# Sums of squares of keys and queries as two-part products with ones, with keys loaded in front of decays and a new engine order, in a delta-rule and stick-breaking trunk

## What is computed

```python
def l2_normalize(x):
    return x * lax.rsqrt(jnp.sum(x * x, axis=-1, keepdims=True) + EPS)
...
q = l2_normalize(heads(qkv[..., :GDN_WIDTH]))
k = l2_normalize(heads(qkv[..., GDN_WIDTH:2 * GDN_WIDTH]))
...
o = gated_delta_chunked(q, k, v, g, beta)
```

## Time and profile before

| what | value |
|---|---|
| median of 3 runs | 3022.31 us (3021.44 to 3025.32) |
| the profiled execution's own time | 3021.47 us |
| its span in the trace | 3019.8 us |
| PE busy | 2962.4 us, 98% |
| PEld busy | 2680.4 us, 89% |
| DVE, ACT, POOL busy | 1499.2, 851.0, 446.1 us |
| chunk loop in the trace | from 405 us to about 757 us |
| one iteration of it | 33.4 us |

### The profile page before, as it was taken

The page is one execution under the profiler, slowest core; times in us unless marked ns, Lnnn a source line. Parts: engine busy times, 40 slices in busy tenths (PEclk is TensorE's granted clock), DMA queues, the critical chain, the costliest instruction groups (busy, mean ns, idle before and its releaser), DMA issues.

```text
span 3019.8 us, 47053 instructions
## 1 busy us (share of the span) xinstructions
PE 2962.4 (98%) x19124; PEld 2680.4 (89%) x19124; DVE 1499.2 (50%) x2161; ACT 851.0 (28%) x1521; POOL 446.1 (15%) x505
## 2 busy tenths in 40 slices
PE   8999989999999999999999999999999999999998
PEld 7999978888999999999999997788888888888887
DVE  5777437666434444434346443666643433333434
ACT  4211235555221111111113102566612111111112
POOL 2000145664210000000000001000021000000000
PEclk9999989999999999999999999999999999999999
DMA  3333321121121111111111425555111111111111
GB/s 122 92 92 94 112 72 59 58 65 57 41 63 42 49 42 42 45 52 49 42 49 57 141 85 168 136 116 116 38 49 56 50 47 49 49 49 44 46 42 70
DMA packets 201815, 207.31 MB, mean 69 GB/s; under 512 B 8363, under 2 KB 172348, under 8 KB 201676
## 3 DMA queue, kind: packets, MB, share of 16 engines
q1 hardware_dynamic: 191098, 167.05, 19.1%
q0 software_dynamic: 10368, 38.21, 3.7%
q10 hardware_dynamic: 210, 0.07, 0.0%
HBM read 162.87 MB, written 42.44 MB: 68 GB/s over the span
## 4 chain that ended last, share of the span: by engine, by line
PE 95%; ACT 2%; issue 1%; DVE 1%; POOL 0%; DMA 0%; ACTq 0%; SPq 0%; DVEq 0%; POOLq 0%
PE PS L1833 20%; PE PS L1835 20%; PE PS L1834 20%; PE PS L2264 5%; PE PS L2263 5%; PE PS L2262 5%; PE PS L2385 2%; PE PS L2369 2%; PE PS L2047 1%; PE PS L2027 1%; PE PS L2336 1%; PE PS L2335 1%; PE PS L1974 1%; PE PS L2084 1%; PE PS L2074 1%
## 5 line engine op out<-in xcount | busy, mean ns | idle before, releaser
L1833 PE MATMUL PS<-YH,WL 128*128 128x348 f32 (+1 forms) x3040 | 1039.9, 342 | 4.4 <-DVE WL L1264 3.0
L1834 PE MATMUL PS<-YL,WH 128*128 128x348 f32 (+1 forms) x3040 | 1038.8, 342 | 0.0
L1835 PE MATMUL PS<-YH,WH 128*128 128x348 f32 (+1 forms) x3040 | 1038.3, 342 | 0.0
L1833 PEld LDWEIGHTS PS<-YH,WL 128*128 128x128 f32 x3040 | 572.0, 188 | 45.3 <-DVE WL L1264 3.3
L1834 PEld LDWEIGHTS PS<-YL,WH 128*128 128x128 f32 x3040 | 571.8, 188 | 37.9 <-issue 0.8
L1835 PEld LDWEIGHTS PS<-YH,WH 128*128 128x128 f32 x3040 | 572.8, 188 | 35.7
L1658 DVE TENSOR_TENSOR hT<-PS,hT 128x346 f32<-128x346 f32 (+2 forms) x440 | 251.4, 585 | 178.7 <-PE PS L2264 178.6
L803 POOL TENSOR_TENSOR gact<-gact,rs 128x346 f32<-128x346 f32 (+2 forms) x110 | 118.7, 1079 | 1307.1 <-ACT gact L1106 1307.1
L2262 PE MATMUL PS<-AH,WL 128*128 128x346 f32 (+2 forms) x880 | 308.6, 351 | 1.1 <-DVE AL L1648 1.1
L2264 PE MATMUL PS<-AH,WH 128*128 128x346 f32 (+2 forms) x880 | 308.8, 351 | 0.0
L2263 PE MATMUL PS<-AL,WH 128*128 128x346 f32 (+2 forms) x880 | 308.8, 351 | 0.0
(11 more groups left out here) (283 smaller groups left out, 3702.0 us busy)
## 6 DMA issues: line engine op xcount, KB each, us to landing
raw<-in_ffn_w_gate_up SPq DMA_DIRECT2D x88, 512.0 KB, 3.7
raw<-in_ffn_w_down SPq DMA_DIRECT2D x44, 512.0 KB, 3.6
s_in<-obuf POOLq DMA_DIRECT2D x32, 520.0 KB, 4.4
raw<-in_gdn_w_in SPq DMA_DIRECT2D x32, 512.0 KB, 4.2
Xqk<-s_in SPq DMA_DIRECT2D x10, 832.0 KB, 5.9
raw<-in_w_kv SPq DMA_DIRECT2D x16, 512.0 KB, 3.9
Xv<-s_in SPq DMA_DIRECT2D x10, 416.0 KB, 3.3
gBc<-s_g SPq DMA_DIRECT2D x10, 416.0 KB, 4.3
```

The costliest lines, as they stand in the source:

```text
L1833: pe.matmul(PS[:, bank, 0:n], wl, xh, start=(k == 0), stop=False)
L1834: pe.matmul(PS[:, bank, 0:n], wh, xl, start=False, stop=False)
L1835: m = pe.matmul(PS[:, bank, 0:n], wh, xh, start=False, stop=(k == KT - 1))
```

## The change

Sums of squares. For chunks h = 1 to 9 the two float32 products are replaced by four fp32r products. ACT writes sqh, the high part of the squares (an fp32r tile), straight from Xqk; POOL squares as before and then subtracts sqh, which leaves the low part sql; PE multiplies both parts by onesr, an fp32r tile of ones, and adds them up in PSUM. Chunk 0, whose sums are made beside the input projections, keeps the old products. Through the nested `ExitStack` sql[0] and sql[1] lie on the bytes of sq[0] and sq[1], and sqh lies on the bytes of rr. So `squares_high` waits for the `unit` that reads rr last.

Loads. SP issues Xqk of a chunk in front of gBc.

Order. The lists of POOL, ACT, DVE and PE are written anew. No other operation is added or removed.

```diff
@@ tiles
+            with ExitStack() as b:
+                sql = [b.enter_context(nc.sbuf_tensor(f"sql{g}", [128, 2, GW], F32R)) for g in range(2)]
+                sqh = b.enter_context(nc.sbuf_tensor("sqh", [128, 2, GW], F32R))
             sq = [head_only(f"sq{g}", [128, 2, GW]) for g in range(2)]
             rr = head_only("rr", [128, 2, GW])
...
+            onesr = gdn_const("onesr", [128, 128], F32R)
@@ SP
             for c in range(1, NC):
                 for g in range(2):
+                    sp.wait_ge(cs["kn"][g], c)
+                    sp.wait_ge(cs["sq"][g], c)
+                    if c > 1:
+                        sp.wait_ge(cs["shi"][g], c - 1)
+                sp.dma_start(Xqk[:, :, :], s_in[c, :, 0:16 * C].rearrange("p (t j) -> p t j", j=C)).then_inc(c_load, 16)
+                for g in range(2):
                     sp.wait_ge(cs["eg"][g], c)
                     sp.wait_ge(cs["dm"][g], c)
                 sp.dma_start(gBc[:, :, :], s_g[c:c + 1].broadcast_to([128, 8, C])).then_inc(c_gb, 16)
-                for g in range(2):
-                    sp.wait_ge(cs["kn"][g], c)
-                    sp.wait_ge(cs["sq"][g], c)
-                sp.dma_start(Xqk[:, :, :], s_in[c, :, 0:16 * C].rearrange("p (t j) -> p t j", j=C)).then_inc(c_load, 16)
@@ POOL
+            def squares_low(h, g):
+
+                pool.wait_ge(cs["sq"][g], h + 1)
+                pool.wait_ge(cs["shi"][g], h)
+                pool.tensor_tensor(sql[g][:, :, :], sq[g][:, :, :], sqh[:, :, :].bitcast(F32), ALU.subtract).then_inc(cs["slo"][g], 1)
@@ ACT
+            def squares_high(h, g):
+
+                act.wait_ge(c_load, 16 * (h + 1))
+                if g:
+                    act.wait_ge(cs["kn"][0], h + 1)
+                else:
+                    act.wait_ge(cs["kn"][1], h)
+                src = Xqk[:, :, :].rearrange("p (w h) j -> p w h j", w=2)[:, :, HG * g:HG * g + HG, :]
+                act.activation(sqh[:, :, :].rearrange("p w (h j) -> p w h j", h=HG), src, ACT.Square).then_inc(cs["shi"][g], 1)
...
+            act.activation(onesr[:, :], ones[:, :], ACT.Copy)
+
             for c in range(-1, NC + 1):
@@ PE, key_sums
-                pe.matmul(PS[:, b0, 0:GW], ones[:, :], sq[g][:, 0, :], start=True, stop=True)
-                pe.matmul(PS[:, b0 + 1, 0:GW], ones[:, :], sq[g][:, 1, :], start=True, stop=True).then_inc(cs["ss"][g], 1)
+                if h == 0:
+                    pe.matmul(PS[:, b0, 0:GW], ones[:, :], sq[g][:, 0, :], start=True, stop=True)
+                    pe.matmul(PS[:, b0 + 1, 0:GW], ones[:, :], sq[g][:, 1, :], start=True, stop=True).then_inc(cs["ss"][g], 1)
+                    return
+                pe.wait_ge(cs["slo"][g], h)
+                for w in range(2):
+                    pe.matmul(PS[:, b0 + w, 0:GW], onesr[:, :], sqh[:, w, :], start=True, stop=False)
+                    m = pe.matmul(PS[:, b0 + w, 0:GW], onesr[:, :], sql[g][:, w, :], start=False, stop=True)
+                m.then_inc(cs["ss"][g], 1)
```

More of the change, by code:

```diff
@@ L753, in _ @@
                     mask(c, 2, 1)
+                if head and h:
+                    squares_low(h, 0)
+                if levels:
+                    decayed(c, 1, 0)
+                    decayed(c, 0, 1)
+                    decayed(c, 1, 1)
+                    mask(c, 3, 0)
                     mask(c, 3, 1)
-                    decayed(c, 1, 1)
-                    mask(c, 5, 0)
+                if head and h:
+                    squares(h, 1)
+                    squares_low(h, 1)
                 if tail and t < NC - 1:
@@ L762, in _ @@
                     fade(t, 1)
[L763 to L766, removed]
                 if levels:
                     mask(c, 5, 1)
+                    mask(c, 5, 0)
+                    mask(c, 6, 1)
                     mask(c, 6, 0)
@@ L1546, in _ @@
                 if levels:
-                    add_u(c, 3, 1)
-                if head and h:
-                    unit(h, 1)
-                if head:
-                    scores(h, 0)
+                    add_u(c, 2, 1)
+                if tail and t < NC - 1:
+                    state(t, 0)
+                    state(t, 1)
                 if levels:
@@ L1555, in _ @@
                     lo(0, P_GO.job0 + 1)
+                if head and h:
+                    unit(h, 1)
+                if levels:
+                    add_u(c, 3, 1)
                 if head:
-                    scores(h, 1)
+                    scores(h, 0)
+                if tail:
+                    gated(t, 1)
                 if levels:
-                    add_u(c, 4, 1)
                     add_u(c, 4, 0)
@@ L2145, in _ @@
                     go_chunk(*GO_ORDER[2])
-                if levels:
-                    level_u(c, 0, 0)
-                    level_x(c, 1, 1)
                 if head and h:
@@ L2151, in _ @@
                 if levels:
-                    level_u(c, 1, 1)
+                    level_x(c, 1, 0)
+                    level_x(c, 1, 1)
                 if tail:
                     outputs(t, 0)
+                if tail and t < NC - 1:
+                    to_state(t, 0)
                 if levels:
-                    level_x(c, 2, 1)
-                    level_x(c, 1, 0)
+                    level_u(c, 1, 1)
+                    level_u(c, 1, 0)
                 if tail:
@@ L2173, in _ @@
                 if levels:
-                    level_u(c, 3, 1)
-                    level_u(c, 2, 0)
-                if head:
-                    key_products(h, 0)
+                    level_u(c, 2, 1)
+                    level_x(c, 3, 0)
+                    level_x(c, 3, 1)
                 if c == NC:
@@ L2182, in _ @@
                 if levels:
-                    level_x(c, 3, 0)
+                    level_u(c, 3, 0)
                 if tail:
@@ L2188, in _ @@
                 if levels:
+                    level_u(c, 3, 1)
+                if head:
+                    key_products(h, 0)
+                if levels:
                     level_x(c, 4, 1)
-                    level_u(c, 3, 0)
+                    level_x(c, 4, 0)
                 if head:
@@ L2193, in _ @@
                 if levels:
-                    level_x(c, 4, 0)
+                    level_u(c, 4, 0)
                     level_u(c, 4, 1)
```

118 lines of the change are left out of this document (54 added, 64 removed).

## The result

The changed kernel takes 3040.14 us (median of 16 runs, 3028.27 to 3052.6), the kernel before 3022.89 beside it (16 runs, 3016.15 to 3025.32): ratio 1.0062, 95% interval 1.0051 to 1.0073. It is slower by 17 us; forecast were 3011 and a range of 3003 to 3018.

The account below looks back on a forecast made before the run. PE's own work was taken to bound the chunk loop. Eight times 1.28 + 0.19 - 0.19 us, plus 1.5 at the start, gave 11.7 off 3021.47: 3009.8, stated as a median of 3011; range 3003 to 3018.

Parts of the forecast that it names:

- The products: Sums of squares on PE: eight fp32r products replace eight float32 records, saving 1.28 us per chunk, ends 0.96 and 1.52.
- Rival (d): Sums on PE: an fp32r product behind a float32 one costs 0.35 us, so nearly nothing is won: 3021; chance 0.04.
- The step that failed is POOL's: POOL gains two subtractions of 1.57 us per chunk, 24 of 32 us busy; cost to PE taken as nothing.
- Slack 2.9 us, so nothing is counted: Chain of norm, unit, square and subtraction takes 6.3 us; PE has 9.24 us of work between first and second sums.
- a pause that takes a subtraction whole: POOL's idle 5.09 us before the first fade was to take in one subtraction of 1.57 us.
- Rival (a): POOL's subtractions hold up DVE operations PE waits for, losing 0.5 to 1 us per chunk: 3014 to 3018; chance 0.14.
- The order on PE: Level 4's two groups on strips become adjacent, saving 0.19 us per chunk; other calls on PE cost what they did.
- SP: Xqk load issued earlier and gBc later; both land in time and cost nothing, with 1.7 us to spare at gBc.
- ACT: Two more squares, 1.8 us per chunk; a new PE wait of 0.19 us at level 3's copy, ends 0 and 0.8.
- The ends: Iteration 0 gains 1.5 us, ends of 4 and minus 2; the last levels change by zero, ends of 2 either way.
- Rival (b): Slower: PE waits for squares_low(h, 1) once ACT's square and DVE's unit are both late; example 3033; chance 0.06.
- the two terms of 0.19 that cancelled: Per chunk, 0.19 us gained on PE from level 4's adjacency and 0.19 us lost waiting at level 3's copy.

Follow-up runs that it names:

- order alone: Changed kernel's new engine and SP order with the old float32 sums in every chunk, no high part or subtraction; 3031.18 us, ratio 1.0029 to the kernel before.
- no subtraction: Changed kernel without POOL's subtraction; PE multiplies the high part of the squares twice instead; 3021.01 us, ratio 0.9994 to the kernel before.
- i_u5_pair: h_pool_waits with the two level_u of level 5 adjacent again on PE, and residue(c, 1) ahead of add_u of level 5 on DVE; 3018.61 us.
- l_tail_late: j_tail with three of the four output copies of the last iteration (high on ACT, low on DVE) moved further back; 3013.23 us, ratio 0.9972.
- j_tail: i_u5_pair with the last iteration's output copies, two high on ACT and two low on DVE, moved later in their queues; 3017.13 us, ratio 0.9986.
- g_diff_early: Changed kernel with one DVE call moved: differences(h, 0) directly behind unit(h, 0); 3026.61 us, ratio 1.0007 to the kernel before.
- f_one_input: Changed kernel with the operations of differences reading one SBUF tensor instead of two, the mask left out; 3036.53 us, ratio 1.0046 to the kernel before.
- e_diff_two: Changed kernel with two wide operations in place of the four of each differences(h, g), in the same place; 3051.93 us, ratio 1.0112.
- h_pool_waits: g_diff_early with one more wait: POOL starts decayed(c, 0, 1) only after DVE's gated(t-1, 0); 3021.60 us, ratio 1.0004.

## Why the prediction was wrong

- **The products:** right. 1.28 us per chunk forecast, 1.29 measured (order alone against no subtraction, 33.77 less 32.48). Rival (d) is out: starts 0.19 us apart.
- **The step that failed is POOL's.** "Slack 2.9 us, so nothing is counted" followed only the chain through sqh to the second sums, and that chain did hold: PE never waited for them. It did not ask who works beside POOL once its pause of 5.09 us is filled. I had named the pause "a pause that takes a subtraction whole", but the pause was what let DVE's differences through in 1.03 us. Filled, it made them 5.00. The cost was 1.17 us per iteration, plus the long iterations at 3.8 and 5.0 us.
- **Rival (a)** had the mechanism and not its size. It priced one delay of 0.5 to 1 us per subtraction, and capped the loss below the gain. Measured: each of four operations in a queue is held by itself, 4 us in all, of which PE sees 1.17. The evidence I set against it, that PE did not wait though POOL was busy 20.9 of 33.4 us, is worth nothing where the placing of these 20.9 us changes. The sign that the prediction set for (a), more than 0.5 us of wait per chunk, did appear: 1.03 us, at MB, behind the differences. The ratio of doubled durations in the earlier trace rows was the sign; I should have multiplied it by the number of operations and looked for who is queued behind.
- **The order on PE:** forecast -0.19, measured +0.40. The text looked at level 4, whose groups became adjacent, and said that the other calls "cost what they did". Level 5's groups had been driven apart by a product on the full array: 0.30. What level 4's adjacency gave was not measured by itself.
- **SP:** "Both cost nothing" is refuted for the old order, +0.86 us per iteration without any load being late. I had asked only whether data come too late, not whether a load at another time changes how DVE and POOL meet. What this exchange does in the new order was not measured by itself.
- **ACT:** the new wait of 0.19 us per iteration at the copy of level 3 did not arise. The subtraction was priced at 1.57 us, the size of the squares, and takes 1.95; nothing hung on that.
- **The ends:** the start, iteration 0 included, was forecast -1.5 and came out at +1.6 in one profile (2.0 in front of the first mark, 0.4 less in iteration 0). Three kernels below that differ only in the tail (i_u5_pair, l_tail_late, j_tail) have the first mark at 414.1, 414.8 and 417.2 us, so the start differs by as much from one execution to the next, and its share in the loss stays open. The tail was taken at zero with ends of 2, and came to +5.5: PE's waits there are 6.4 us against 3.9, and the copies for the output stand ahead of what PE wants next. The order alone shows 3.8 of it.
- **Rival (b)**, the slower one, had the right sign for the wrong place. What it asked for (ACT and DVE both late for the second sums) never occurred.

The sum of the loop by these sizes, for the eight iterations behind the first: -10.3 (products) + 3.2 (order) + 9.4 (differences) + 8.8 (what the two long ones have over 33.65) = 11.1 us; the first is 0.4 shorter, so 10.7, against 10.6 measured. That it closes is no proof of its own, since the first three terms are differences of the same periods; the proof of the POOL term is that moving one DVE call (g_diff_early) gives the 1.17 back with all of POOL's work in place, and that POOL's wait takes the long iterations away. With both faults and level 5 repaired the period is 32.18, where 32.1 was forecast, and with the tail repaired the kernel takes 3013.23, within the range given. That is another kernel, so it does not make the forecast right; and that the period comes so near is in part luck, since of the two terms of 0.19 that cancelled in the sum the wait did not arise and the gain was not measured. The forecast was of a kernel whose queues do not meet; this one's do.

## What to carry to other kernels

A pause on GpSimd can be what lets VectorE's SBUF work through. Before filling one, list VectorE's operations beside it, count them (here the number mattered more than the width), price each at the whole GpSimd operation that it meets, as a loss that can come and need not, and follow who is queued behind. Two cheap repairs worked: move the block next to GpSimd's idle time, or make GpSimd wait for it.

## What the runs showed of the hardware

- The hold is per instruction and whatever its size: 104x4 elements took 0.15 us alone, 0.68 and 1.11 beside POOL's row; two wide operations in place of four narrow ones took 3.50 us instead of 5.00.
- It isn't always one POOL operation: `o<-o,ro` of 0.6 us was held for 2.78 until three of them had ended (557.14 to 559.92), and the same two lengths, 2.78 and 2.94 us within 0.02, came back in the long iterations of four kernels (changed, g_diff_early, f_one_input, e_diff_two). Why it is once 0.7 and once 2.8 us stays open.
- POOL is held as well, and an unbroken row does not always win: in the kernel before a mask of 0.59 us took 1.07 beside `o<-o,ro`, which kept its 0.59; in the changed kernel `U<-NT,lvl` takes 1.84 us beside `gated(t, 1)`, against 1.07 before. The order of the starts in the records doesn't tell who is held: in h_pool_waits `dec` starts at 491.43, beside a mask that ends at 491.63, and POOL's square at 491.59; `dec` ends behind the square, after 1.86 us instead of 0.32.
- DVE operations that take an operand from PSUM (`MB<-PS,M`, `S<-PS,S`) kept their 0.25 and 0.68 us beside the same row.
- A wait of PE of 2.55 us was followed 2.6 us later by 3.4 us at 1.2 GHz, so a wait can cost more than its length. The spread of the changed kernel's runs, 24 us against 9, would fit a varying number of such iterations; that was not counted over runs.
